# Eight of the early weight units of the first network: their low parts computed by GpSimd instead of VectorE

## The reference, cut to what matters

```python
c_act = jax.nn.silu(c)
mod = c_act @ w_ada[l] + b_ada[l]                       # (1, 9 * 2048)
sh1, sc1, g1, sh2, sc2, g2, sh3, sc3, g3 = jnp.split(mod, N_MOD, axis=-1)
hn = _modulate(_rms(h, norm_ffn1[l]), sh1, sc1)         # rms * (1 + sc1) + sh1
h = h + 0.5 * g1[:, None, :] * _swiglu(hn, ffn1_w1[l], ffn1_w3[l], ffn1_w2[l])
...                                                     # mixer, then a second network of the same form
```

## Time and profile before

| what | value |
|---|---|
| runs, median | 2477.75 us (2476.37 to 2479.46) |
| profiled execution, its own time | 2477.61 us |
| its span | 2475.7 us |
| PE busy | 2452.0 us, 99% |
| DVE busy | 1885.9 us, 76% |
| ACT busy | 1183.2 us, 48% |
| POOL busy | 166.7 us, 7% |
| chain that ended last | PE 94%, DVE 3%, DMA 3% |

### The profile page before, as it was taken

One profiled execution on the slowest core, in us unless ns is written; L12 is line 12 of the kernel. 1 busy time (PEld: TensorE's weight loads), 2 busy tenths in 40 slices (PEclk: granted clock), 3 DMA queues, 4 the chain that ended last, 5 costly groups with the idle time before them and its releaser, 6 DMA issues.

```text
span 2475.7 us, 33524 instructions
## 1 busy us (share of the span) xinstructions
PE 2452.0 (99%) x12264; PEld 2081.1 (84%) x12264; DVE 1885.9 (76%) x2117; ACT 1183.2 (48%) x1477; POOL 166.7 (7%) x268
## 2 busy tenths in 40 slices
PE   7999999999999999999999999999999999999999
PEld 5888888888888999898888888888988888888887
DVE  6886679898988988888987777776889655555556
ACT  4444444444446655755556444344644444444443
POOL 4210000000000001111100000000000000000000
PEclk9999999999999999999999999999999999999999
DMA  9986679999986889985654888796699776777775
GB/s 371 377 293 190 193 246 365 308 371 311 358 291 221 274 282 321 305 279 171 182 150 145 267 270 295 257 315 243 204 331 324 213 212 208 209 211 211 209 211 176
DMA packets 290421, 641.74 MB, mean 259 GB/s; under 512 B 26002, under 2 KB 26868, under 8 KB 289396
## 3 DMA queue, kind: packets, MB, share of 16 engines
q1 hardware_dynamic: 269744, 571.41, 70.2%
q0 software_dynamic: 18800, 64.00, 7.8%
q10 hardware_dynamic: 1748, 4.62, 0.5%
HBM read 622.06 MB, written 17.88 MB: 258 GB/s over the span
## 4 chain that ended last, share of the span: by engine, by line
PE 94%; DVE 3%; DMA 3%; issue 0%; ACT 0%; ACTq 0%; POOL 0%; DVEq 0%
PE psum L2533 26%; PE psum L2534 26%; PE psum L2535 26%; PE psum L2841 3%; PE psum L2843 3%; PE psum L2842 3%; PE psum L2895 2%; DMA raw<-in_ffn_w 2%; PE psum L2521 1%; DVE w_lo L1564 1%; DVE ada_acc L1678 1%; PE psum L2872 1%; PE psum L2874 1%; PE psum L2873 1%; DMA badas<-in_b_ada 0%
## 5 line engine op out<-in xcount | busy, mean ns | idle before, releaser
L1016 ACT ACTIVATE w_hi<-raw 128x1024 fp32r<-128x1024 f32 (+1 forms) x850 | 897.6, 1059 | 1009.2 <-PE psum L2535 795.8
L1564 DVE TENSOR_TENSOR w_lo<-raw,w_hi 128x1024 fp32r<-128x1024 f32 (+1 forms) x850 | 1034.1, 1221 | 452.7 <-ACT w_hi L1016 451.2
L2533 PE MATMUL psum<-w_hi,xT_hi 128*128 128x512 f32 x1920 | 752.7, 392 | 4.5 <-issue 3.4
L2534 PE MATMUL psum<-w_lo,xT_hi 128*128 128x512 f32 x1920 | 748.7, 390 | 0.0
L2535 PE MATMUL psum<-w_hi,xT_lo 128*128 128x512 f32 x1920 | 748.4, 390 | 0.0
L2533 PEld LDWEIGHTS psum<-w_hi,xT_hi 128*128 128x128 f32 x1920 | 361.3, 188 | 83.3 <-issue 8.8
L2535 PEld LDWEIGHTS psum<-w_hi,xT_lo 128*128 128x128 f32 x1920 | 361.2, 188 | 75.8
L2534 PEld LDWEIGHTS psum<-w_lo,xT_hi 128*128 128x128 f32 x1920 | 361.5, 188 | 73.0
L1584 DVE SCALAR_TENSOR_TENSOR ada_acc<-ada_raw,cact,ada_acc 128x1024 f32<-128x1024 f32 x210 | 268.9, 1280 | 3.1 <-DMA ada_raw<-in_w_ada 3.0
L2533 PE MATMUL psum<-w_hi,aT_hi 128*128 128x512 f32 x688 | 268.5, 390 | 0.0
L2535 PE MATMUL psum<-w_hi,aT_lo 128*128 128x512 f32 x688 | 267.8, 389 | 0.0
(11 more groups left out here) (315 smaller groups left out, 2243.1 us busy)
## 6 DMA issues: line engine op xcount, KB each, us to landing
raw<-in_ffn_w SPq DMA_DIRECT2D x528, 512.0 KB, 4.6
ada_raw<-in_w_ada SPq DMA_DIRECT2D x224, 512.0 KB, 6.2
raw<-in_w_in SPq DMA_DIRECT2D x224, 512.0 KB, 4.5
ada_raw<-in_w_ada POOLq DMA_DIRECT2D x32, 512.0 KB, 7.0
ada_more<-in_w_ada POOLq DMA_DIRECT2D x32, 512.0 KB, 7.5
raw<-in_w_br_ssd SPq DMA_DIRECT2D x32, 512.0 KB, 5.3
raw<-in_w_br_att SPq DMA_DIRECT2D x32, 512.0 KB, 4.4
raw<-in_w_out SPq DMA_DIRECT2D x32, 512.0 KB, 5.3
```

The source lines that it names most:

```text
L1016: nc.scalar.activation(w_hi[:, n.slot(SPLIT), 0:size], raw[:, n.slot(RAW), 0:size], ACT.Copy).then_inc(hi_ready, 1)
L1564: nc.vector.tensor_tensor(w_lo[:, n.slot(SPLIT), 0:size], raw[:, n.slot(RAW), 0:size], w_hi[:, n.slot(SPLIT), 0:size], ALU.subtract).then_ ...
L2533: nc.tensor.matmul(o, hi[:, kt + k, toks], whi, start=a, stop=False)
L2534: nc.tensor.matmul(o, hi[:, kt + k, toks], wlo, start=False, stop=False)
```

## The change

The low parts of units 9, 13, 17, 21, 25, 29, 33 and 37 are taken by GpSimd, between its loads of pieces: after the load of piece `min(SPLIT_AFTER[n] + 5, 63)`. A new semaphore `pool_low` counts them. TensorE waits for it at those units, and SyncE waits for it before the raw load of the unit that reuses the slot. VectorE leaves these eight out, and its signal after the next unit counts two.

```diff
+POOL_LOW = (9, 13, 17, 21, 25, 29, 33, 37)
...
+    pool_low = sem("pool_low")
...
-            if n.n0 >= RAW:
+            if n.n0 - RAW in POOL_LOW:
+                sp.wait_ge(pool_low, POOL_LOW.index(n.n0 - RAW) + 1)
+            elif n.n0 >= RAW:
                 sp.wait_ge(split_ready, n.count(plus=1 - RAW))
             sp.dma_start(as2(raw[:, s, :]), source).then_inc(raw_in[s], 16)
...
+        def low(n):
+            pool.wait_ge(hi_ready, n + 1)
+            nc.gpsimd.tensor_tensor(w_lo[:, n % SPLIT, :], raw[:, n % RAW, :], w_hi[:, n % SPLIT, :],
+                                    ALU.subtract).then_inc(pool_low, 1)
+
+        low_after = {min(SPLIT_AFTER[n] + ADA_AHEAD - 1, PIECES - 1): n for n in POOL_LOW}
         for m in range(ADA_DEEP + 2, PIECES):
             load_first(m)
+            if m in low_after:
+                low(low_after[m])
...
             nc.vector.tensor_tensor(w_lo[:, n.slot(SPLIT), 0:size], raw[:, n.slot(RAW), 0:size],
-                                    w_hi[:, n.slot(SPLIT), 0:size], ALU.subtract).then_inc(split_ready, 1)
+                                    w_hi[:, n.slot(SPLIT), 0:size], ALU.subtract).then_inc(
+                                        split_ready, 2 if n.n0 - 1 in POOL_LOW else 1)
 
         def sub_units(upto):
             while done[0] < upto:
-                sub(At(done[0]))
+                if done[0] not in POOL_LOW:
+                    sub(At(done[0]))
                 done[0] += 1
...
-            pe.wait_ge(split_ready, n.count(plus=1))
+            if n.n0 in POOL_LOW:
+                pe.wait_ge(pool_low, POOL_LOW.index(n.n0) + 1)
+            else:
+                pe.wait_ge(split_ready, n.count(plus=1))
```

## The result

The changed kernel takes 2485.35 us (median of 11 runs, 2480.94 to 2490.26) against 2478.03 us before on the same chips: 7.3 us or 0.3% slower, ratio 1.0027 with a 95% interval of 1.0019 to 1.0034. The prediction was 2478.6 us, range 2475.8 to 2483.2. The profiled execution took 2487.94 us, its span is 2486.1 us, so it is one of the longer ones.

A forecast was written before the change was run, and what follows sets the result against it. The prediction took TensorE, DMA and VectorE as all near their limit from 80 to 160 us, with TensorE bounding what follows. Only unit 25's late low part counted: 2477.61 + 1.0 = 2478.6 us, range 2475.8 to 2483.2.

The forecast's parts named there:

- What bounds the kernel, and what can be won: From 64 to 170 us TensorE and DMA set the pace; relieving VectorE wins at most 0.8 us.
- What a subtraction costs on GpSimd: Each moved subtraction of 1024 columns takes 2.2 us on GpSimd, with bounds of 0.89 and 3.9 us.
- Unit 25, +1.0 us: GpSimd ends unit 25's low part at 118.2 instead of VectorE's 117.25; TensorE waits for it, so +1.0 us.
- its 0 for the held-back raw load: SyncE's raw load for unit 25 is queued up to 1.4 us later but joins a full DMA queue: taken as 0.
- gives up eight subtractions ... 9.1 us less for VectorE: VectorE loses eight subtractions of 1.14 us each, 9.1 us less work, all beside TensorE's stream.
- a rival with 0.32: GpSimd and VectorE block each other when GpSimd reads and VectorE's instruction has two inputs: 2481.1 us, chance 0.32.
- The signs that the prediction had set: Wrong if TensorE waits over 4 us; blocking if L946 reaches 3.5 us and TensorE waits for VectorE at units 35, 39.
- The rival's price: Blocking: 1.06 us lost per moved subtraction, delays at units 25, 35 and 39 of 1.6, 1.1 and 0.8, sum 3.5 us.
- a drop of the clock: Addition to blocking: after a pause seven matmuls start at the 1.2 GHz spacing, 1.4 us more, making 2482.5 us.
- Units 29, 33 and 37: nothing: GpSimd's low parts for these units are ready within TensorE's margins, so they add nothing.
- What else is moved: Later piece loads, raw loads and the memset of y are hidden or taken as 0.
- Held-back loads did not starve the last set: Rival: delayed piece loads make VectorE wait and the last set close late, 2484 us and more; chance 0.05.

The follow-up runs named there:

- experiment 4: The kernel before, with VectorE's eight subtractions (units 9, 13, ... 37) cut to 8 of 1024 columns and nothing put on GpSimd: 2479.54 us, ratio 0.9999.
- experiment 1: The changed kernel, with each of GpSimd's eight subtractions replaced by two memsets of about the same total time that only write: 2478.75 us, ratio 1.0001.
- Experiments 1 and 3: The second of the two: the kernel before, VectorE unchanged, plus eight GpSimd memsets of 2784 columns that nobody waits for: 2477.05 us, ratio 0.9993.
- experiment 9: The kernel before plus eight GpSimd copies of 2560 columns from h to y, reading one tile, that nobody waits for: 2489.2 us, ratio 1.0041.
- experiment 10: The changed kernel with only the subtractions of units 29, 33 and 37 on GpSimd: 2482.92 us, ratio 1.0016.
- the first four alone: The changed kernel with only the subtractions of units 9, 13, 17 and 21 on GpSimd: 2480.0 us, ratio 1.0007.

## Why the prediction was wrong

**What bounds the kernel, and what can be won: right.** TensorE's stream and the DMA engines set this stretch; relieving VectorE of 8 x 1.14 us moves nothing that the times show (experiment 4).

**What a subtraction costs on GpSimd: right in size.** 2.34 to 2.41 us where it ran undisturbed, 2.2 forecast, within the bounds of 0.89 and 3.9 us.

**Unit 25, +1.0 us: the right size, but half of the delay there.** GpSimd began at 117.01 and ended at 119.36; TensorE went on at 119.49 instead of 117.38, and waited 2.06 us. Of the 2.1 us 1.1 are the subtraction, the other 0.94 are a cast that was itself later (116.92 against 115.98). In experiment 1, where nothing is stopped, that cast was not late (it began at 114.72 against 114.92), although unit 21's slot came free 2.2 us later than before (104.7 against 102.5), and TensorE went on at 118.45, 1.07 us late. So, as far as one trace of each shows, the sum's +1.0 is what the change costs without the block, its 0 for the held-back raw load was right, and the 0.94 come with the block. The chain of waits of the changed kernel there:

```profile
111.97 1.07 ACT w_hi L1028
...
114.20 1.29 DVE ada_acc L1692
...
117.01 2.35 POOL w_lo L946
...
119.49 0.47 PE psum L2550
```

**The step that failed: "gives up eight subtractions ... 9.1 us less for VectorE".** The sum had no term for what GpSimd's reads take from VectorE. It was written down as a rival with 0.32 and priced apart, when it is a plain part of the cost: 2.0 to 2.5 us stopped at seven of the eight units and 0.5 at unit 17, about 16 us in all, against eight times 1.14, 9.1 us, given back. VectorE did not gain 9 us, it lost 7. The rule of the Trainium skill (SBUF, State Buffer, Who interferes with whom) was on the table, and it said just this: two inputs in SBUF on VectorE, a GpSimd instruction that reads SBUF, the later one fully blocked. Here the runs agree with it: 3.74 us beside GpSimd's subtraction, 1.28 beside its memset; which of the two is held they show only roughly (units 17 and 33 above). I weighed against it that VectorE's subtractions were even to 12 ns beside GpSimd's loads and a memset. Experiments 1 and 3 show that this evidence could not bear on the matter, since GpSimd read nothing in that stretch before; and by experiment 9 it need not read two tiles. The signs that the prediction had set came: TensorE waited 6.7 us in all from 64 to 170 us, over the 4 us that it had named as the sign of being wrong; the subtraction took up to 3.65 us; and TensorE waited for VectorE at unit 35 (0.37 us), and 1.84 us at unit 36 in place of unit 39.

**The rival's price: right mechanism, under half of the size without the clock.** It forecast 3.5 us (2481.1), 4.9 with a drop of the clock; the measured loss is 7.3. Three things make up the difference, and they can be read off one place, unit 36. Two were missing in the rival's sum, the third, the clock, stood beside it with 1.4 us. Before, its low part was ready at 148.3 and TensorE took it at 121.91 + 10 x 2.73 = 149.2. VectorE's subtractions of units 26 and 36 in the kernel before:

```profile
118.35 1.22 DVE L1564 TENSOR_TENSOR w_lo<-raw,w_hi 128x1024 fp32r<-128x1024 f32 x1
...
147.08 1.22 DVE L1564 TENSOR_TENSOR w_lo<-raw,w_hi 128x1024 fp32r<-128x1024 f32 x1
```

and in the changed kernel, with the long piece beside unit 29's subtraction between them:

```profile
120.36 1.21 DVE L1576 TENSOR_TENSOR w_lo<-raw,w_hi 128x1024 fp32r<-128x1024 f32 x1
...
130.34 3.43 DVE L1692 SCALAR_TENSOR_TENSOR ada_acc<-ada_raw,cact,ada_acc 128x1024 f32<-128x1024 f32 x1
...
154.01 1.21 DVE L1576 TENSOR_TENSOR w_lo<-raw,w_hi 128x1024 fp32r<-128x1024 f32 x1
```

The chain of waits of the changed kernel there (it shows the subtraction from where the piece before it ends):

```profile
150.33 3.75 DVE ada_acc L1692
154.09 1.15 DVE w_lo L1576
...
155.37 0.47 PE psum L2550
```

First, VectorE itself was 2.0 us late behind unit 25 (unit 26's subtraction at 120.36 instead of 118.35); the rival made TensorE late there and left VectorE on time. Second, a block takes effect before its relief: at unit 36 VectorE had been stopped for units 29, 33 and 37 (2.15 + 2.46 + 2.47 = 7.1 us, the last being the 3.75 us row), and relieved of only 29 and 33 (2.3 us). 2.0 + 7.1 - 2.3 = 6.8 us, and its subtraction is 6.9 us later than before (147.08 to 154.01). I had looked at units 35 and 39 and not at the one between. TensorE's margin of 0.9 us off that leaves 6.0; 155.37 against 149.2 is 6.2. Third, behind the pause the clock was at 1.2 GHz: seven times in a row the matmuls start 0.43 instead of 0.23 us apart, and once 0.40, 1.6 us in all. Two of them:

```profile
156.35 0.63 PE L2550 MATMUL psum<-w_hi,xT_hi 128*128 128x512 f32 x1
156.78 0.63 PE L2551 MATMUL psum<-w_lo,xT_hi 128*128 128x512 f32 x1
```

6.2 + 1.6 is the 7.8 us by which the fold is late in this trace.

**"Units 29, 33 and 37: nothing".** True of GpSimd's own results (TensorE waited 0.35 us for unit 29, and for none of the others), wrong of what they cost VectorE: experiment 10 has these three at about 4 us.

**What else is moved: mostly right.** No piece was waited for. Held-back loads did not starve the last set, and in experiments 1 and 3 they cost nothing. One thing stays open: the cast of unit 17 came 2.6 us later than before (91.44 against 88.83) although its raw load could start no later. TensorE waited 1.42 us there. In experiment 1 that cast ended at 91.06, 2.2 us late, so it does not come of the block; why the data was late no run tells, and with the first four alone it was not.

**Ranges.** The range ended at 2483.2 because the rival's own end (2484) was cut and its share above 0.2% was put at a fourth. With the block in the sum as the rival had it, the centre would have been at 2481.1, and even the rival's own end lies under the measured 2485.35.

## What to carry to other kernels

Work moved from VectorE to GpSimd is not free for VectorE when both have their operands in the same on-chip memory: count GpSimd's whole duration as time stopped for VectorE (2.46 us against the 1.14 us that the subtraction had cost it), unless GpSimd only writes, or VectorE is waiting at that moment anyway (0.5 us lost at unit 17). Before an engine is relieved, cut the work out altogether in one run: if that gains nothing, no cheaper place for the work will gain either. And walk a price through every instruction that stands between a block and its relief, not only those at the ends.

## What the runs showed of the hardware

- A GpSimd instruction that reads, with one input or two, stops VectorE's two-input instructions for nearly its whole length (2.0 to 2.5 us here, of 2.3 to 2.4); one that only writes for as long (2.45 us) does not, and neither does the issue of loads (0.72 us each).
- TensorE's clock went to 1.2 GHz behind pauses of 1.84 and 1.86 us and held behind others of 1.56, 2.06 and 2.17 us: the length of a pause in this range does not tell.
- Short GpSimd instructions behind each other take turns with VectorE's in some places (four quarters of 0.72 us needed 6.63 and 6.99 us) and ran on end at others (2.82 us at unit 37, with one VectorE instruction stopped for all of it).
- VectorE's first piece of a set, a TENSOR_SCALAR with one input, was stopped as well. It takes 0.75 us alone; at 77.57 us in the changed kernel, beside the subtraction of unit 13, it took 3.19:

```profile
77.83 2.38 POOL L946 TENSOR_TENSOR w_lo<-raw,w_hi 128x1024 fp32r<-128x1024 f32 x1
```

```profile
77.57 3.19 DVE L1690 TENSOR_SCALAR ada_acc<-ada_raw,cact 128x1024 f32<-128x1024 f32 x1
```
